# A recurrence on chunks of 64 tokens instead of 32 in a hybrid decoder layer

## The reference

```
S = S * w_t + (S a_t) b_t^T + v_t k_t^T        # per head, a 64 x 64 state
y_t = S r_t
# a_t = -kk, b_t = kk * alpha;  then y is normed over the 64 features of a head,
# scaled, a bonus is added and the sum is multiplied by a gate
```

## Time and profile before

| | |
|---|---|
| three runs | 2328.8 us median (2324.08 to 2337.22) |
| profiled execution, span | 2329.1 us |
| PE busy | 2231.0 us, 96% |
| VectorE busy | 1756.5 us |
| ScalarE busy | 1141.8 us |
| GpSimd busy | 1025.4 us |
| projection | 0 to 549 us |
| recurrence | 549 to 859 us |

### The profile page before, as it was taken

The page is one execution under the profiler, slowest core; times in us unless marked ns, Lnnn a source line. Parts: engine busy times, 40 slices in busy tenths (PEclk is TensorE's granted clock), DMA queues, the critical chain, the costliest instruction groups (busy, mean ns, idle before and its releaser), DMA issues.

```text
span 2329.1 us, 43634 instructions
## 1 busy us (share of the span) xinstructions
PE 2231.0 (96%) x16652; PEld 1816.6 (78%) x16652; DVE 1756.5 (75%) x1910; ACT 1141.8 (49%) x1795; POOL 1025.4 (44%) x726
## 2 busy tenths in 40 slices
PE   7999999996999979998999999999999999999998
PEld 6777777775878768887888888788788888887886
DVE  3756798994884466769989999666799898976565
ACT  5646556452445554444444444454554444444543
POOL 4636466571234335535776766100146555541000
PEclk9999999998999989999999999999999999999999
DMA  7364556347567547895434343677733332326774
GB/s 203 93 227 134 178 160 209 106 140 216 154 166 194 144 144 234 268 279 166 153 119 147 121 146 128 217 252 255 237 119 115 104 111 93 113 95 202 247 260 145
DMA packets 435819, 395.61 MB, mean 170 GB/s; under 512 B 59548, under 2 KB 352076, under 8 KB 432332
## 3 DMA queue, kind: packets, MB, share of 16 engines
q1 hardware_dynamic: 407804, 343.06, 47.8%
q10 hardware_dynamic: 27856, 50.34, 6.0%
HBM read 266.97 MB, written 126.35 MB: 169 GB/s over the span
## 4 chain that ended last, share of the span: by engine, by line
PE 55%; DVE 3%; DMA 2%; ACT 1%; issue 1%; SPq 0%; ACTq 0%; POOLq 0%; POOL 0%; DVEq 0%
PE late_bank L133 18%; PE late_bank L134 18%; PE late_bank L135 18%; DVE wt_lo L2906 1%; DMA scratch_a<-p_keep 1%; ACT wt_hi L2727 1%; PE late_bank L2199 1%; DMA o_lo<-scratch_q 0%; DVE wt_lo L2860 0%; DMA p_keep<-in_w_down 0%; DMA raw<-in_w_down 0%; DMA scratch_x<-x_tile 0%; DMA p_keep<-scratch_td 0%; DVE p_ub L2869 0%; DVE x_tile L2168 0%
## 5 line engine op out<-in xcount | busy, mean ns | idle before, releaser
L133 PE MATMUL late_bank<-o_hi,wt_hi 128*128 128x512 f32 x1232 | 481.3, 391 | 8.0 <-DVE o_lo L2962 3.3
L134 PE MATMUL late_bank<-o_lo,wt_hi 128*128 128x512 f32 x1232 | 480.7, 390 | 0.0
L135 PE MATMUL late_bank<-o_hi,wt_lo 128*128 128x512 f32 x1232 | 480.6, 390 | 0.0
L431 POOL TENSOR_TENSOR p_w_lo<-p_w_raw,p_w_hi 128x1024 fp32r<-128x1024 f32 x72 | 190.4, 2645 | 221.2 <-ACT p_w_hi L502 221.2
L133 PEld LDWEIGHTS late_bank<-o_hi,wt_hi 128*128 128x128 f32 x1232 | 232.0, 188 | 58.7 <-issue 7.2
L135 PEld LDWEIGHTS late_bank<-o_hi,wt_lo 128*128 128x128 f32 x1232 | 232.1, 188 | 48.8
L134 PEld LDWEIGHTS late_bank<-o_lo,wt_hi 128*128 128x128 f32 x1232 | 232.0, 188 | 47.8
L2597 POOL TENSOR_TENSOR tsum<-raw 128x512 f32<-128x512 f32 x43 | 106.2, 2469 | 358.5 <-DVE p_ub L2947 179.4
L133 PE MATMUL p_ppr<-p_hT_hi,p_w_hi 128*128 128x512 f32 x576 | 233.4, 405 | 0.2 <-ACT p_ring L513 0.2
L133 PE MATMUL late_bank<-wt_hi 128*128 128x512 f32 x572 | 223.2, 390 | 7.2 <-DVE wt_lo L2906 6.6
L135 PE MATMUL p_ppr<-p_hT_hi,p_w_lo 128*128 128x512 f32 x576 | 226.6, 393 | 0.0
(11 more groups left out here) (328 smaller groups left out, 4679.3 us busy)
## 6 DMA issues: line engine op xcount, KB each, us to landing
raw<-in_w_up SPq DMA_DIRECT2D x88, 512.0 KB, 5.1
p_w_raw<-in_w_in SPq DMA_DIRECT2D x72, 512.0 KB, 3.9
scratch_a<-p_keep SPq DMA_DIRECT2D x22, 1280.0 KB, 4.5
raw<-scratch_a SPq DMA_DIRECT2D x96, 256.0 KB, 3.0
raw<-scratch_td SPq DMA_DIRECT2D x52, 256.0 KB, 3.7
p_keep<-scratch_a SPq DMA_DIRECT2D x47, 256.0 KB, 2.9
scratch_a<-p_keep SPq DMA_DIRECT2D x44, 256.0 KB, 2.0
raw<-in_w_down SPq DMA_DIRECT2D x44, 256.0 KB, 4.1
```

The source lines that it names most:

```text
L133: nc.tensor.matmul(out, lhs_hi, rhs_hi, start=start, stop=False, skip_group_check=again)
L134: nc.tensor.matmul(out, lhs_hi, rhs_lo, start=False, stop=False, skip_group_check=again)
L135: return nc.tensor.matmul(out, lhs_lo, rhs_hi, start=False, stop=stop, skip_group_check=again)
L431: nc.gpsimd.tensor_tensor(w_lo[i][:, :, :], w_raw[i][:, :, :], w_hi[i][:, :, :].bitcast(F32), ALU.subtract).then_inc(s_wl, 1)
```

## The change

Chunks of the recurrence are 64 tokens long (`L = 2 * C`), two in an iteration. The 32 x 32 inverses stay as they are; those of a chunk's two halves become the diagonal blocks of a 64 x 64 inverse, and its corner is X1 L21 X2, made by three small products per head and chunk: `corner`, `corner_right`, `corner_left`, with reads by ScalarE between, and X1 transposed by VectorE. w is gone: PE computes A S onto z in PSUM, ScalarE reads p, PE applies the inverse, ScalarE reads u. b and k are stored by the projection in the compact layout in which the recurrence reads them, a and r together, bonus and gate together; a is no longer transposed in the projection (`a_rows`, L899 with `p_dec`). Centring and scaling of y go from VectorE to GpSimd; `mo` and the bonus and gate tiles get two buffers. The blocks of inverses are solved in 6 gaps over 5 iterations, before in 8 over 4.

```diff
 def store_rk(b):
-    for key, at, ready, done in (("rt", R0, s_rt, s_rst), ("kt", K0, s_kt, s_kst)):
-        sp.wait_ge(ready, ONE + b + 1)
-        sp.dma_start(scr[key][:, :, bass.ds(b * TB, TB)], um[:, at:at + PAIRS, :]).then_inc(done, 16)
+    sp.wait_ge(s_rt, ONE + b + 1)
+    sp.dma_start(kind("ar", b, 1), tokens(um[:, R0:R0 + PAIRS, :])).then_inc(s_rst, 16)
+    sp.wait_ge(s_kt, ONE + b + 1)
+    for c in range(2):
+        sp.dma_start(chunk_kind(b, c, 1 - c), chunks(um[:, K0:K0 + PAIRS, :], c)).then_inc(s_kst, 16)
...
 def small(b, pair):
-    if pair == 0 and b > 0:
-        pe.wait_ge(s_abr, ONE + b)
-        rows(dec, [pm[:, g, :] for g in range(TT)], s_atn)
...
 # SyncE, the inverses of one group
-    for q in range(4):
-        sp.dma_start(xt[g][C * q:C * q + C, :, q % 2, :], view[g, q // 2, q % 2][bass.ds(k, 1)].rearrange("b s d t -> (b s) d t")
-                     ).then_inc(s_xt[g], 16)
+    for c in range(2):
+        for e in range(2):
+            sp.dma_start(xt[g][quad(c, e), :, C * e:C * e + C], whole[k, g, c, e]).then_inc(s_xl[n % 2], 16)
+            for h in range(2):
+                sp.dma_start(xd[n % 2][quad(c, h), e, :, :], parts[k, g, c, h, e]).then_inc(s_xl[n % 2], 16)
...
 # PE
 def from_state(c2):
+    for j in range(PAIRS):
+        for h in range(2):
+            last = nc.tensor.matmul(pbank[urows(c2), h, j, :], ar[now][half(h), j, 0, c2 * L:c2 * L + L],
+                                    st[p][c2][half(h), j, :], start=False, stop=True, skip_group_check=True)
+def inverse(c2):
+    for h in range(2):
+        pe.wait_ge(s_p, ONE + i * 4 + c2 * 2 + h + 1)
+        for j in range(PAIRS):
+            u = h * PAIRS + j
+            last = nc.tensor.matmul(ubank[urows(c2), h, j, :], xt[now][urows(c2), u, :], pz[urows(c2), u, :],
+                                    start=True, stop=True, skip_group_check=True)
+        last.then_inc(s_xp, 1)
+def to_state(c2):
+    for h in range(2):
+        pe.wait_ge(s_u, ONE + i * 4 + c2 * 2 + h + 1)
+        for j in range(PAIRS):
+            last = nc.tensor.matmul(bank[half(h), SB, j * H:(j + 1) * H], bkt[p][:, c2, j * P + h * H:j * P + h * H + H],
+                                    uv[now][:, c2, h * PAIRS + j, :], start=True, stop=True)
+def z(c2):
+    for h in range(2):
+        for j in range(PAIRS):
+            last = nc.tensor.matmul(pbank[urows(c2), h, j, :], am[q][vrows(c2), h, j, :], uv[nxt][vrows(c2), c2, h * PAIRS + j, :],
+                                    start=j == 0, stop=True, skip_group_check=True)
...
+def corner(o, u):
+    h, c2, j = u % 2, u // 2 % 2, u // 4
+    return nc.tensor.matmul(o[quad(c2, h), j * C:(j + 1) * C], ar[nxt][half(h), j, 0, c2 * L + C:c2 * L + L],
+                            kinds[half(h), j, c2, c2 * L:c2 * L + C], start=True, stop=True)
+def corner_right(o, u):
+    h, c2, j = u % 2, u // 2 % 2, u // 4
+    return nc.tensor.matmul(o[quad(c2, h), j * C:(j + 1) * C], l21[quad(c2, h), j, :], xd[q][quad(c2, h), 1, j, :],
+                            start=True, stop=True)
+def corner_left(h):
+    for j in range(PAIRS):
+        for c2 in range(2):
+            at = (h * PAIRS + j) * C
+            last = nc.tensor.matmul(bank[quad(c2, 0), ROT[t], at:at + C], x1u[quad(c2, h), j, :], m1[quad(c2, h), j, :],
+                                    start=True, stop=True)
+def grams_r(c2, second, done):
+    for j in range(PAIRS):
+        for h in range(2):
+            last = nc.tensor.matmul(gbank(second)[:, h, j, :], kinds[half(h), j, c2, :],
+                                    ar[nxt][half(h), j, 1, c2 * L:c2 * L + L], start=True, stop=True)
...
 # VectorE and GpSimd, y
-        nc.vector.tensor_tensor(yv, yv, stat[:, 0, :].unsqueeze(2).to_broadcast([P, DBL, H]), ALU.add).then_inc(s_yc, 1)
+        nc.gpsimd.tensor_tensor(y[n % 3][:, :, :], y[n % 3][:, :, :], stat[p][:, 0, :].unsqueeze(2).to_broadcast([P, HEADS, H]),
+                                ALU.add).then_inc(s_yc, 1)
```

More of the change, by code:

```diff
@@ L37 @@
 CH = SC // C
+L = 2 * C
+HEADS = 2 * PAIRS
 UNITS = PAIRS * CH
@@ L652, in _ @@
                             high_w(n + WB)
-                        if f == 1 and b > 0:
-                            a_rows(b - 1, [pm[:, g, :] for g in range(TT)])
                         if f == 2:
@@ L1038, in phase_recur, with several @@
         FIRST = BLOCKS - 2
-        def two(name, shape):
-            return [sb(f"{name}{i}", shape) for i in range(2)]
-        ar = [scr["first_ar"], scr["ar1"]] + [sb(f"ar{i}", [P, 2, PAIRS, SC]) for i in range(2, BATCH)]
-        bt = scr["first_bt"]
-        kt = scr["first_kt"]
-        bonus = sb("bonus", [P, PAIRS, SC])
-        gate = sb("gate", [P, PAIRS, SC])
+        GAPS = 6
+        TURNS = 5
+        PARTS = GAPS * (TURNS - 1) + 3
+        def several(name, n, shape):
+            return [sb(f"{name}{i}", shape) for i in range(n)]
@@ L1062, in phase_recur @@
+        xd = [scr["xd0"], scr["xd1"]]
+        x1u, l21 = scr["x1u"], scr["l21"]
+        m1 = sb("m1", [P, PAIRS, C])
+        pz = sb("pz", [P, HEADS, H])
+        y = several("y", 3, [P, HEADS, H])
+        mo = several("mo", 2, [P, PAIRS, SC])
+        inv, above, prod = scr["solve"], scr["above"], scr["prod"]
+        st = [[sb(f"st{p}{c}", [P, PAIRS, H]) for c in range(2)] for p in range(2)]
         sumst = sb("sumst", [P, PAIRS, H])
-        y2 = sb("y2", [P, DBL, H])
-        stat = sb("stat", [P, 4, DBL])
@@ L1118, in phase_recur @@
         s_sd = sem("y_deviation")
+        s_rec = sem("y_deviation_recip")
+        s_yc2 = sem("y_normed")
         s_add = sem("bonus_added")
         s_mo = sem("mix_ready")
-        s_mix = sem("mix_stored")
-        s_mixb = sem("mix_in_b_place_stored")
+        s_mix = [sem(f"mix{i}_stored") for i in range(2)]
         s_third = sem("third_mix_loaded")
@@ new lines, in grams_first @@
+                    def grams_first():
+                        pe.wait_ge(s_gm, ONE + 3 * (i + 1))
+                        for j in range(PAIRS):
+                            for c2 in range(2):
+                                for h in range(2):
+                                    last = nc.tensor.matmul(gbank(False)[vrows(c2), h, j, :], kinds[half(h), j, c2, (1 - c2) * L:(2 - c2) * L],
+                                                            ar[nxt][half(h), j, 0, c2 * L:c2 * L + L], start=True, stop=True)
+                        grams_r(0, True, s_ga)
@@ L1692, in from_r @@
                         for j in range(PAIRS):
-                            for c4 in range(CH):
-                                last = nc.tensor.matmul(ybank[C * c4:C * c4 + C, j * 2 + h2, :], old[half(h2), 1, j, c4 * C:c4 * C + C],
-                                                        st[q][c4][half(h2), j, :], start=h2 + j == 0, stop=True, skip_group_check=True)
-                        last.then_inc(s_yd if h2 else s_yh, 1)
+                            for c2 in range(2):
+                                last = nc.tensor.matmul(ybank[urows(c2), j * 2 + h, :], ar[old][half(h), j, 1, c2 * L:c2 * L + L],
+                                                        st[q][c2][half(h), j, :], start=h + j == 0, stop=True, skip_group_check=True)
@@ L1698, in from_uv @@
+                        last.then_inc(s_yd if h else s_yh, 1)
                     def from_uv():
                         for j in range(PAIRS):
-                            for h2 in range(2):
-                                for c4 in range(CH):
-                                    nc.tensor.matmul(ybank[C * c4:C * c4 + C, j * 2 + h2, :], ark[slot - 2][:, j * CH + c4, h2 * C:h2 * C + C],
-                                                     uv[slot - 2][:, c4, j, :], start=False, stop=True, skip_group_check=True)
```

733 lines of the change are left out of this document (315 added, 418 removed).

## The result

The changed kernel takes 2389.5 us (median of 4 runs, 2385.2 to 2390.9) against 2329.5 for the kernel before on the same chip: 1.0255 of it, 95% interval 1.023 to 1.0281. The forecast was 2314 us, in 2292 to 2349. It is slower by 60 us where 15 us faster was expected.

A forecast was written before the change was run, and what follows sets the result against it. The recurrence was taken as bound by PE's issue. Projection -5.6 and -2.5, second iteration's start -0.8, iterations -6.4, last iteration -1.8 and end +2 summed to -15.1: 2314 us, range 2292 to 2349.

The forecast's parts named there:

- Projection: Stage before the recurrence: 8.1 us shorter, -5.6 from a's dropped transposes in three blocks and -2.5 in the fourth.
- DMA: 16,400 packets, I take 0, upper end +2 per block: Projection's short-run stores: 13 to 39 us of sixteen engines per block of about 135 us, taken as no loss.
- Iteration: Recurrence, one pass: 15.57 us of PE work plus 0.65 of waits, 16.2 instead of 16.66; -6.4 over 14.
- X groups: PE's two applications of the inverse X per iteration, 16 records each in one tile: 2.16 us together.
- rival C: Better overlap in the recurrence: cheaper narrow records, no 0.14 us between neighbouring groups, waits hidden; 2299 us, chance 0.15.
- grams with r: PE in each iteration, twice 16 records alternating in two row tiles: 1.22 us together.
- rival B: Row halves don't alternate with 64 columns, so state products and grams cost 2.4 us more per iteration; 2348, chance 0.12.
- Rival A: No gain in the recurrence: ScalarE's reads and SyncE's DMAs show, iteration 17.3 us, total 2329; chance 0.21.
- rival D: PE's stands lower the clock: above 2440 us, or 2339 if one iteration in five; or small stores, +8; chance 0.07.
- VectorE never the last to arrive: Sign in the recurrence: VectorE 8 to 12 us busy per iteration, and PE never held up by it.
- Start: Recurrence's start: parameters some 4 us later behind 12 small DMAs, first state product at about 571 instead of 568.37.
- Wrong if the first PE work of the recurrence comes after 563: Sign against the forecast: PE's first work in the recurrence starting later than 563 us in the trace.

The follow-up runs named there:

- e5: Changed kernel with all six tensors stored in 2 KB runs, norm parameters loaded earlier and the second system solved later: 2336.0 us.
- e1: Changed kernel with b and k stored in 2 KB runs as before and split on the loading side: 2367.1 us.
- e2: Kernel before the change, with only b and k stored in 256-byte runs and loaded accordingly: 2358.1 us.
- e3: Changed kernel with its layout, b's two stores issued apart, at column tiles of the next block (last block: tiles 16 and 17): 2363.1 us.
- e12: Changed kernel with six added 128 x 128 transposes per iteration and nothing else: 2377.8 us.
- e6: e5 with six added 128 x 128 transposes of the identity per iteration, where PE waits: 2329.6 us.
- e8: e5 with both the six added transposes and the third solving piece moved behind the first state update: 2312.8 us.
- e10: e8 with the six added transposes cut to 32 x 32 elements: 2326.3 us.
- e13: e11 with 32 unread 128 x 128 products put ahead of the recurrence's loop: 2308.2 us.
- e14: e13 with 18 added transposes instead of 6 per iteration while i < 2: 2305.0 us.
- e7: e5 with the third piece of VectorE's solving moved behind the first state update: 2328.3 us.
- e4: Changed kernel with norm parameters loaded ahead of the inverse's blocks and the second system's solving started later: 2378.1 us.
- e9: e5 with GpSimd's two passes over y cut to one column each, so y isn't normed: 2328.8 us.
- e11: e8 with VectorE's solving started three gaps later: 2313.4 us.

## Why the prediction was wrong

- *Projection, -8.1 forecast, +28.3 measured: the step that failed.* The PE part was right in its direction, and too small: e5, without the stores' effect, ends the stage 12.2 us ahead of the kernel before; why it is 4 more is open. The step "DMA: 16,400 packets, I take 0, upper end +2 per block" asked only whether sixteen engines could move them. What it needed is the issue time of ScalarE's queue, ahead of the bank reads. The earlier trace rows shows a store's 0.37 us alone, and no row of before could price a store behind one of 2048 runs, since there is none; but b's 1.42 us behind the bonus's 0.59 was a hint, and the program lines up vT, bonus, twice b and a there. Issuing b cost 12 us per block instead of 1.4. e1, e2 and e3 show it three ways: -22, +27, -26 us. The sixteen engines were not the main bound: e3 moves the same short runs. So the rule on runs under 512 bytes was not needed for the main part of the loss.
- *Iteration, 16.2 forecast, 15.38 measured at full clock.* Right in kind, mis-sized in parts. The X groups took 0.87 us (1.08 forecast), the state updates 0.90 (1.08), z about 1.5 (2.03), each left corner 0.37 (0.49): neighbouring groups overlap at their ends, as rival C said. The grams with r took 1.04 (0.61): rival B's mechanism, for this group alone, while the state products had their 0.61. The waits were 0.38 and 0.35 (0.65 together), on the copies named. Rival A's 17.3 us did not come: the plain iteration has 15.38.
- *Clock, rival D, chance 0.07: the second failure.* The text argued that a wait of 0.87 us had left the clock up, so waits under 1 us were safe. They were safe in that place of before, not here. A row of before would have warned: there too the clock fell once in mid-loop, behind waits of only 0.82 and 1.49 us (the second is in the first line, from the timeline; the window behind it, without a hole in PE, has 0.50):

```profile
640.86 0.66 PE L1706 MATMUL late_bank<-p_ident,bk 128*128 128x128 f32 x4 [1.49 <-ACT p_mo L1446]
```

```profile
643.00:649.00 6.00, 6.00 (x113) 5.59 (x115) 3.91 (x6) 2.55 (x7) 3.73 (x5) 0.50 0.77 216
```

  The changed stage has 108 us at the half clock, 79 more than before. PE works in 90 of them (25 before); at half speed that is some 33 us more, and without it the stage would be about 12 us shorter than before's (333.4 - 45 against 312.6 - 12.5, an estimate from the profiles). Rival D had the place right. Its size for the clock was 2339, 25 us over the forecast, if one iteration in five lost it (the +8 there is for the small stores), and its chance, 0.07, was far too low. e12, e6, e8, e10, e13 and e14 carry this; e7 and e4 show that removing long waits alone isn't enough.
- *"VectorE never the last to arrive": wrong.* 2.61 us at i = 3, 3.27 at i = 5. The plan of gaps was priced at 0.4 us a step. GpSimd's new passes over y, taken as free since y is wanted an iteration later, stretch steps to 1.1 to 1.2 us and push others under the sums with bonus and gate, where they take 1.3 to 1.45 (e5, e9); and the load of the second system had lost its slack (e4).
- *Start: 22.3 us from the stage's first instruction to the first state product forecast (571 - 548.7), 26.3 measured, 19.7 before.* Right cause, two and a half times the size (+6.6 instead of +2.6). With the parameters first it is 18.8 (e5: 536.48 to 555.32).
- *Wrong if the first PE work of the recurrence comes after 563*: it came at 589, for the most part because the projection ended 28 us late.
- *The later stages* are 5.3 us longer, with 29 instead of 18 us of half clock; in e8 they take 1468.1, as before. Why is open.

e8's 2312.8 us lie beside the forecast of 2314, and that is in part luck. Against before, its profiled execution has the projection 12.5 us shorter (8.1 forecast) and the recurrence 7.3 shorter (7.0 forecast), but the latter with iterations of 15.5 us instead of 16.2 and 60 us at the half clock, with stores in 2 KB runs, and with added products that the forecast didn't have.

## What to carry to other kernels

Price a DMA also at its issuer: count the stores that are already in that engine's queue and their runs, and look at which work of the engine stands behind. When large products are replaced by many small ones, look at the granted clock window by window, and try a few large products in the holes; here six per iteration were worth 6 to 16 us. When work moves to GpSimd because it is idle, ask what VectorE does at that moment.

The best version is e14: 2305.0 us, 0.9883 of the kernel before (0.9855 to 0.991) and 84 us under the changed one.

## What the runs showed that was not expected

- A store of 2048 runs of 256 bytes issues in 0.52 us with nothing issued for 22 us before it, in 1.02 directly behind one like it, and in 7.06 behind two others (e3); one of 512 runs takes 1.46 us behind two stores of 512 runs (e5), and 8.10 where the nearer of the two has 2048 (e1).
- TensorE ran at 1.2 GHz for 24 us without a hole (e13, 563 to 587) and for some 32 us with 0.6 us of holes (e11). The Trainium skill, "TensorE: Matmul & The Clock Gate", Why this matters for your kernels, advises against longer idle gaps between bursts of matmuls, which cost clock. Here that was not enough: behind gaps of only 0.84 and 0.97 us the clock came down, and it stayed down without any (e13), and with more large products that nobody reads it stayed up (e14: 1.00 in the same window).
- Added work made the program faster: six 128 x 128 transposes per iteration 15.5 us (e7 to e8), six of 32 x 32 2 us, within the scatter.
